# A four-layer diffusion block on one core: where the first layer's conditioning is computed, and the order of weight splits at norms and in the convolution

## The reference, cut to what matters

```python
mx = jnp.split((silu_c @ ada_w[i] + ada_b[i])[:, None, :], 6, axis=-1)   # latent tokens; mc with silu_cc for context
hx = modulate_norm(xs, norm_mix[i], mx[0], mx[1])    # rms_norm(x, gain) * (1 + scale) + shift
yx, yc = mixer_i(hx, hc)
xs = xs + mx[2] * yx
hx = modulate_norm(xs, norm_ffn[i], mx[3], mx[4])
xs = xs + mx[5] * conv_ffn(hx, ...)                  # the same for the context, but in the last layer
```

## Time and profile before

| | us |
|---|---|
| median of 3 runs | 2446.84 (2445.07 to 2448.78) |
| the profiled execution | 2448.26 |
| its span in the profile | 2446.1 |
| busy: PE / DVE / ACT / POOL | 97% / 73% / 42% / 27% of the span |
| mean granted PE clock | 0.993 of full speed |
| DMA | 346.20 MB, mean 142 GB/s |

### The profile page before, as it was taken

How to read it: one execution, slowest core, us unless ns; L and a number is a source line. 1 busy time by engine, 2 the same in 40 slices (tenths; PEclk the granted TensorE clock), 3 DMA queues, 4 the chain that set the end, 5 groups by cost and what they waited for, 6 DMA issues and landing times. The chain is left out here.

```text
span 2446.1 us, 35542 instructions
## 1 busy us (share of the span) xinstructions
PE 2381.3 (97%) x12398; PEld 1951.9 (80%) x12398; DVE 1782.1 (73%) x2667; ACT 1025.6 (42%) x1557; POOL 657.2 (27%) x445
## 2 busy tenths in 40 slices
PE   8998999999999999999999999999999999998999
PEld 6874688888888878888888888668888887867999
DVE  5777788888974355428988777988988775556774
ACT  4356434443232334314444325554444323555543
POOL 2553433333200030022333225843333224101000
PEclk9999999999999999999999999999999999999999
DMA  8550235446633311223555544523554545312556
GB/s 301 166 187 1 70 117 178 163 160 215 207 101 110 99 67 61 95 95 138 171 175 174 178 152 124 148 79 138 172 174 160 185 159 136 122 44 74 190 184 190
DMA packets 104648, 346.20 MB, mean 142 GB/s; under 512 B 13232, under 2 KB 22896, under 8 KB 104544
## 3 DMA queue, kind: packets, MB, share of 16 engines
q1 hardware_dynamic: 72656, 240.26, 29.4%
q10 hardware_dynamic: 28656, 95.16, 12.0%
q0 software_dynamic: 3232, 9.38, 1.8%
HBM read 334.96 MB, written 1.05 MB: 137 GB/s over the span
## 5 line engine op out<-in xcount | busy, mean ns | idle before, releaser
L1680 DVE TENSOR_TENSOR Wlo<-raw,Whi 128x1024 fp32r<-128x1024 f32 x424 | 637.5, 1504 | 268.6 <-ACT Whi L1266 264.9
L1266 ACT ACTIVATE Whi<-raw 128x1024 fp32r<-128x1024 f32 x424 | 448.4, 1060 | 810.0 <-DMA raw<-in_weights 712.7
L748 PE MATMUL bank<-Hhi,Whi 128*128 128x512 f32 (+1 forms) x2136 | 763.3, 357 | 12.5 <-DVE Hlo L1756 5.4
L749 PE MATMUL bank<-Hlo,Whi 128*128 128x512 f32 (+1 forms) x2136 | 755.8, 354 | 0.0
L750 PE MATMUL bank<-Hhi,Wlo 128*128 128x512 f32 (+1 forms) x2136 | 755.7, 354 | 0.0
L748 PEld LDWEIGHTS bank<-Hhi,Whi 128*128 128x128 f32 x2136 | 404.7, 189 | 78.0 <-issue 12.6
L750 PEld LDWEIGHTS bank<-Hhi,Wlo 128*128 128x128 f32 x2136 | 404.7, 189 | 55.3
L749 PEld LDWEIGHTS bank<-Hlo,Whi 128*128 128x128 f32 x2136 | 404.8, 190 | 55.0
L608 POOL TENSOR_TENSOR cond_w<-cond_w,cond 128x1024 f32<-128x1024 f32 x111 | 270.3, 2435 | 556.8 <-DVE square L1704 510.9
L748 PE MATMUL bank<-Ghi,Whi 128*128 128x512 f32 (+1 forms) x770 | 268.3, 348 | 0.9 <-DVE Wlo L1680 0.9
L749 PE MATMUL bank<-Glo,Whi 128*128 128x512 f32 (+1 forms) x770 | 267.3, 347 | 0.0
(11 more groups left out here) (278 smaller groups left out, 2871.0 us busy)
## 6 DMA issues: line engine op xcount, KB each, us to landing
raw<-in_weights SPq DMA_DIRECT2D x424, 512.0 KB, 3.4
cond_w<-in_ada ACTq DMA_DIRECT2D x176, 512.0 KB, 4.1
ada_raw<-in_ada SPq DMA_DIRECT2D x16, 512.0 KB, 15.0
rel_in<-in_rpb POOLq DMA_DIRECT2D x48, 128.0 KB, 5.8
shifted<-U SPq DMA_DIRECT2D x84, 66.0 KB, 2.1
decay_t<-in_dist POOLq DMA_DIRECT2D x4, 640.0 KB, 4.2
X<-in_x SPq DMA_DIRECT2D x4, 512.0 KB, 5.9
shifted<-U ACTq DMA_DIRECT2D x28, 66.0 KB, 2.1
```

The source lines that it names most:

```text
L748: t.matmul(dst, Whi[:, st.slot, w], hi, start=start, stop=False)
L749: t.matmul(dst, Whi[:, st.slot, w], lo, start=False, stop=False)
L1266: a.activation(Whi[:, st.slot, :], raw[:, st.slot, :], ACT.Copy).then_inc(hi_split, 1)
L1680: v.tensor_tensor(Wlo[:, st.slot, :], raw[:, st.slot, :], Whi[:, st.slot, :].bitcast(F32), ALU.subtract)\
```

## The change

Six edits. (1) The 18 hosted slices of layer 0's QKV product become 20, all made by DVE alone; ACT and POOL lose their part. (2) The output projection hosts four slices instead of six. (3) At the entries of layers 1 and 2 (r = 2, 4), DVE scales chunks 2 and 3 ahead of the weight split and makes the low parts behind it, and PE takes the first two chunks of its first tile before it waits for the second tile's split. (4) At the entry of layer 3 (r = 6) the three splits stand one behind each pair of chunks. (5) In the convolution, sigmoid and gate of chunk 1 are moved ahead, the sigmoid among ACT's products of chunk 0, the gate ahead of DVE's last addition of chunk 0. (6) At the start, ACT makes the high part of chunk 2 before the split, not after it.

```diff
-HOSTED = ((0, 0, 0, 0), (0, 1, 1, 1), (1, 1, 1, 0), (1, 1, 1, 1), (1, 1, 1, 1), (1, 1, 1, 1))
+HOSTED = ((0, 0, 0, 0), (0, 1, 1, 1), (1, 1, 1, 1), (1, 1, 1, 1), (1, 1, 1, 1), (2, 1, 2, 0))
-IN_OUT = 6
+IN_OUT = 4
-ALONE = sum(HOSTED[1]) + sum(HOSTED[2])
         def shared(n):
-            return ALONE <= n < IN_SLICES or any(p["hosts"] and p["cond_up"] <= n < p["cond_down"] for p in layers)
+            return any(p["hosts"] and p["cond_up"] <= n < p["cond_down"] for p in layers)
...
@@ POOL, pairs_staged
-                if layer == 0:
-                    pool.wait_ge(cond_ready, 2)
-                    for n in range(ALONE, IN_SLICES):
-                        scale_weights(n)
@@ PE, three_tiles
+                early = 2 if r % 2 == 0 else 0
+                for k in range(early):
+                    pe.wait_ge(h_ready, ready + k + 1)
+                    three(bank[0][:, CT], steps[0], slice(P * k, P * k + P), Hhi[:, k, CT], Hlo[:, k, CT], k == 0, False)
                 pe.wait_ge(lo_split, steps[1].n + 1)
                 for k in range(C):
                     pe.wait_ge(h_ready, ready + k + 1)
-                    for m in range(2):
+                    for m in range(1 if k < early else 0, 2):
@@ ACT, norm_apply
-                high(r, 0, 4, 6)
-                split(following[1])
+                if r == 2 * DEPTH - 2:
+                    split(following[1])
+                    high(r, 0, 4, 6)
+                    split(following[2])
+                else:
+                    high(r, 0, 4, 6)
+                    split(following[1])
                 high(r, 0, 6, C)
-                for st in following[2:]:
-                    split(st)
@@ ACT, na: hosts and the last sum
-                            if n > ALONE:
-                                sum_products(n - 1)
-                    sum_products(IN_SLICES - 1)
@@ ACT, conv: sigmoid(c) is a function now
-                    act.wait_ge(weights_used, steps[1].n + 1)
-                    a.activation(glu_s[:, k, :], bank[2 * k + 1][:, :], ACT.Sigmoid,
-                                 bias=cvb[:, 1, c:c + 1]).then_inc(glu_sigmoid, 1)
+                    if c != 1:
+                        sigmoid(c)
...
                     for n, tap in enumerate(pool_taps[c]):
+                        if c == 0 and n == 5:
+                            sigmoid(1)
@@ ACT, start
+            first_high(2)
             split(Step(2 - LEAD))
-            first_high(2)
@@ DVE, normed_chunks(r, half, first, end, between=None)
-                    if c > first:
+                    if c > first and between is None:
                         low(c - 1)
+                if between is not None:
+                    split(between)
+                    low(end - 2)
                 low(end - 1)
@@ DVE, norm_halves
                 normed_chunks(r, 0, 0, 4 if r % 2 else 2)
-                if r % 2 == 0:
+                if r == 2 * DEPTH - 2:
                     split(following[0])
-                    normed_chunks(r, 0, 2, 4)
+                elif r % 2 == 0:
+                    normed_chunks(r, 0, 2, 4, following[0])
                 dve.wait_ge(weights_used, following[1].n + 1)
                 add_half(tiles[-1], bank[6], 1, XT, tile_free)
-                normed_chunks(r, 0, 4, C)
-                split(following[1])
-                for st in following[2:]:
-                    split(st)
+                if r == 2 * DEPTH - 2:
+                    for n in range(1, 4):
+                        normed_chunks(r, 0, 2 * n, 2 * n + 2)
+                        if n < 3:
+                            split(following[n])
+                else:
+                    normed_chunks(r, 0, 4, C)
+                    split(following[1])
@@ DVE, conv
-                    gate(c)
+                    if c != 1:
+                        gate(c)
+                    else:
+                        dve.wait_ge(tap_done, taps_before[c])
...
-                    if c == C - 2:
-                        gate(C - 1)
+                    if c in (0, C - 2):
+                        gate(c + 1)
```

More of the change, by code:

```diff
@@ L1531, in conv, with sigmoid @@
                 act.wait_ge(cos_loaded, 32)
+                def sigmoid(c):
+                    act.wait_ge(weights_used, p["mix"] + 2 * c + 2)
+                    a.activation(glu_s[:, c % 2, :], bank[2 * (c % 2) + 1][:, :], ACT.Sigmoid,
+                                 bias=cvb[:, 1, c:c + 1]).then_inc(glu_sigmoid, 1)
                 for c in range(C):
@@ L1745, in norm_scale, with normed_chunks @@
                 dve.wait_ge(scale_ready, r + 1)
-            def normed_chunks(r, half, first, end):
+            def normed_chunks(r, half, first, end, between=None):
                 layer, part = r // 2, r % 2
```

## The result

Six runs of the changed kernel gave a median of **2433.11 us** (2428.84 to 2435.19), six of the kernel before 2447.62 us (2445.07 to 2449.91). The ratio is 0.9939, 95% interval 0.9926 to 0.9952: 14.5 us faster. The profiled execution took 2433.01 us, its span 2431.2. The forecast was 2427.0, range 2422 to 2436: sign and range hold, but of the 19.8 us forecast 14.5 came. Where the other 5 went is the question of what follows.

What follows compares the result with a forecast made beforehand. It took TensorE as the bound, busy 2381.3 of 2446.1 us, with gain only from its waits and low clock. Gains of 5.0 + 8.8 + 1.7 + 4.3 = 19.8 us gave 2427.0 us against the median; range 2422 to 2436.

Steps and rivals of the forecast that it cites:

- no stretch of low clock between 20 and 1600: Sign that the forecast is right: PE's clock is never low from 20 to 1600 us.
- the third scoring step: Sign in layer 0: PE starts this step behind V near 175 us, 3.4 us earlier than the 178.40 before.
- Part 1: Layer 0's QKV loop with hosted slices on VectorE alone: gain 5.0 us, bounds 0 and 6.5.
- part 6: Order at the start: PE gains 1.0 us at 33.5 but waits the same later; 0, bounds 0 and 1.0.
- VectorE has no time left: Rival in layer 0's QKV loop: its 59.6 us in 61 hold no waits, three long passes lose the gain; 2432, chance 0.12.
- Part 2: Four slices in the output projection: the 5.6 us wait and low clock behind it go; gain 8.8 us, bounds 4 and 10.
- Part 3: Norms at the entries of layers 1 and 2: gain 0.7 + 1.0 us, bounds 0.5 and 2.5.
- part 4: Entry of layer 3, splits placed between pairs of chunks: gain 4.3 us, bounds 2 and 6.
- Part 5: Convolution, gate and sigmoid hoisted: the wait only moves on to a later split; 0, bounds -1.7 and +1.8.
- the clock falls anyway: Rival at the FFN entry or in the convolution, behind a wait near 2.4 us: costs 1.7 to 4, 2430, chance 0.11.

Runs made afterwards that it cites:

- the kernel with the moved slice: Changed kernel with one hosted slice moved from the last quarter of the second weight slice to the quarter ahead of it: 2426.20 us, ratio 0.9915.
- the hoist undone: Changed kernel with sigmoid and gate of chunk 1 in the convolution back at their old places: 2429.85 us, ratio 0.9935.

## Why the prediction was right, and where it was not

**What bounds the kernel.** Right: all of the gain came out of PE's waits and the low clock behind them, at the places read from the profile. PE was idle 64.8 us of the span before and 55.5 after, and its busy time fell by 5.6. Of the signs set down, "no stretch of low clock between 20 and 1600" failed twice, at 96.3 and 1523.1, and the third scoring step came at 178.89, not near 175, since PE was done with V at 176.1 and not at 171.5.

**Part 1, forecast 5.0.** The reasoning about the loop held, nearly to the number: DVE would be done 1.3 us ahead of PE, and in the kernel with the moved slice it was 1.10; the third scoring step would start 3.5 us behind the end of V, and it started 2.8 us behind (170.46 to 173.24); the stage gave 5.9 us there (182.3 less 176.4). With sharing left in, the output projection began 8.7 us later. In the changed kernel it gave 4.3, and 3.0 had been lost ahead of it. With the hoist undone, where the code up to the convolution is that of the changed kernel and the clock did not fall, it gave 5.9 as well (269.48 less 93.03 is 176.45).

**The step that failed is part 6**, "0; bounds 0 and 1.0". Its PE side came true (the wait of 0.98 us at 33.5 went, and the one at 41.9 grew from 0.23 to 1.42). But the step was followed on ACT and PE only. POOL waits for the very rows that came 1.04 us sooner, and what it then does are 24 loads and 16 additions, beside a weight load and DVE's passes. The bound left out a loss, with no reason that excluded one. In this pair the stage ahead lost 3.0 us and, with the 1.6 of the low clock behind it (178.0 less 176.4), 4.6. Some 1.9 of the 3.0 are the order's by the mean of the profiles; the rest is a weight group that landed late. By the medians the loss is not settled: undoing edit 6 gave 2.5 us in the changed kernel, with the moved slice it came out slower, and edit 6 alone cost the kernel before nothing. The sentence in part 1 that "POOL's queue holds nothing else here" was right for the time behind 98 us and was not asked for the time ahead of it. The rival "VectorE has no time left" was near in kind, but named the end of the loop, and there DVE had time.

**Part 2, forecast 8.8, measured 7.9.** The wait did not go whole: POOL's total was ready 0.5 us after PE asked, where 0.4 to spare was worked out. The next wait was 0.70, as put. What is left for the clock is 7.9 - (5.6 - 0.5) + 0.7 = 3.5 us, against 3.9 from the row. By the rule of the Trainium skill (TensorE: Matmul & The Clock Gate, "HAM oscillation — how this bites in real kernels") it would have been 5.1, an estimate. The row was nearer, since PE was idle in 2.4 of the 10.2 us at the low level (318.6 to 321.0).

**Part 3, forecast 1.7, measured 2.1; part 4, forecast 4.3, measured 4.35.** Both right in this pair. But the kernel with both undone shows that 4.35 is right only against an execution in which the clock fell, so this agreement is in part luck.

**Part 5, forecast 0, measured -1.2** in this pair, inside its bounds. The wait moved on to where it was said to go, at 2.15 us for the 2.4 forecast, and the clock fell there, as the rival "the clock falls anyway" has it, but it cost 0.6 us and not 1.7 to 4. Over thirteen profiles the forecast of 0 stands.

Together: 19.8 less 3.7 (parts 1 and 6), 1.2 (part 5) and 0.9 (part 2), plus 0.9 (part 3, the rest), is 14.9 us in the span. That this lies in the range is not owed to part 6: the range's upper end was made for shortfalls of parts 1 and 2. Its lower end, 2422, is said to be two thirds of the upper bounds of parts 1 to 4; these add up to 25 us, and it takes all of them to come to 2422, while two thirds give 2430.

## What to carry to other kernels

When a step is moved by a microsecond, look up every semaphore that it feeds, on all engines: the cost may lie 50 us later, in another engine's transfers and port. A late engine costs nothing while another one bounds its stage, so a change that moves the bound also gives a price to waits that had none. A part worth a microsecond or two is not read from medians that scatter by 2.5 us, but from the step between two marks that repeats over many profiles. Work that can stand in an engine's idle time belongs ahead of the transfer that the idle time waits for, not behind it.

## What the runs showed of the hardware that was not expected

**The clock's fall is not settled by the wait.** In the fourteen profiles of this case all 12 waits of PE of 2.58 to 5.61 us behind the first 20 us came with the lower clock, which began during the wait or just behind it. Of 33 waits of 2.08 to 2.53 us, 14 did; the 2.27 us at the entry of layer 3 did in two of three, a wait of 2.13 us at the FFN entry of layer 3, which all fourteen have, in three. And all fourteen had a low stretch at the convolution's end, where no wait was over 2.24 us (1.50, 0.40 and 0.27 us in the kernel before, ahead of the fall at 1615.7).

What a fall cost differs too. It was 1.4 to 2.4 us behind the early wait (from there to the output projection it took 177.8 to 178.8 us with it, 176.4 or 176.5 in the three profiles without it and without another wait), and 0.3 to 1.0 in the convolution. At the entry of layer 3 it was 3.5 with one low stretch and 3.8 with two, against the kernel without; 2.1 and 1.5 of that is a later wait for normed rows, which that kernel did not have. So a wait near 2.2 us has two prices, and one profile shows only one of them.

**Small loads beside a large one.** A weight group of 512 KB landed 3.1 us after its issue when POOL's second batch was held back, and 9.3 to 11.8 us after it in the thirteen profiles with that batch of twelve loads of 128 KB around it. How many of the twelve were issued ahead of it, four to twelve, shows no relation to the time.
